# Raw weights in transfers of two blocks, 1 MB each, in place of single blocks of 512 KB

## What is computed

```python
def first_block(x, c, ...):
    for layer in range(2):
        shift_m, scale_m, gate_m, shift_f, scale_f, gate_f = ada_mod(c, ada_w[layer], ada_b[layer])
        h = modulate(rms_norm(x, norm_gains[layer, 0]), shift_m, scale_m)
        y = attn_hybrid_mixer(h, ...) if layer % 2 == 0 else retention_mixer(h, ...)
        x = x + gate_m * y
        h = modulate(rms_norm(x, norm_gains[layer, 1]), shift_f, scale_f)
        x = x + gate_f * swiglu(h, ffn_w_gate_up[layer], ffn_w_down[layer])
    return rms_norm(x, final_norm)

def second_block(x, ...):
    for l in range(2):
        x = hybrid_layer(x, ...)   # convolution, latent attention and dilated attention, gated and merged
    return x
```

## Time and profile before

| | |
|---|---|
| median of 3 runs | 1480.45 us (1480.04 to 1490.38) |
| the profiled execution's own time | 1489.58 us |
| its span, first to last instruction | 1487.6 us |
| TensorE busy | 98% of the span |
| VectorE busy | 70% |
| ScalarE busy | 57% |
| GpSimd busy | 6% |
| mean traffic | 196 GB/s |
| granted TensorE clock, mean | 0.996 of full speed |

### The profile page before, as it was taken

One profiled execution on the slowest core, in us unless ns is written; L12 is line 12 of the kernel. 1 busy time (PEld: TensorE's weight loads), 2 busy tenths in 40 slices (PEclk: granted clock), 3 DMA queues, 4 the chain that ended last, 5 costly groups with the idle time before them and its releaser, 6 DMA issues.

```text
span 1487.6 us, 30216 instructions
## 1 busy us (share of the span) xinstructions
PE 1462.6 (98%) x11596; PEld 1379.8 (93%) x11596; DVE 1037.8 (70%) x1835; ACT 854.3 (57%) x1458; POOL 85.7 (6%) x136
## 2 busy tenths in 40 slices
PE   8999999999999999999999999999999999999999
PEld 6887999999989899999998989889999898989999
DVE  2878888898696666555675857876676674787665
ACT  4565666545456656655566766554566676655553
POOL 0101000110000000000020000220000000021000
PEclk9999999999999999999999999999999999999999
DMA  9966688898574355655663555336666355423663
GB/s 361 329 209 205 224 291 289 291 379 311 186 283 146 123 186 166 185 183 185 186 231 117 164 163 161 96 92 196 194 193 218 103 173 168 149 91 111 191 197 126
DMA packets 81183, 292.02 MB, mean 196 GB/s; under 512 B 9185, under 2 KB 10465, under 8 KB 80946
## 3 DMA queue, kind: packets, MB, share of 16 engines
q1 hardware_dynamic: 68274, 244.31, 50.5%
q0 software_dynamic: 11792, 42.77, 8.7%
q10 hardware_dynamic: 1008, 3.41, 0.7%
HBM read 289.40 MB, written 1.05 MB: 195 GB/s over the span
## 4 chain that ended last, share of the span: by engine, by line
PE 89%; DVE 5%; ACT 3%; issue 2%; DMA 1%; SPq 0%; DVEq 0%; ACTq 0%
PE G L495 22%; PE G L497 22%; PE G L496 22%; PE G L554 2%; PE G L556 2%; PE G L555 2%; DVE wlo L1546 2%; PE O L1037 1%; PE S L1006 1%; PE Tp L962 1%; PE G L576 1%; PE Tp L890 1%; ACT whi L1091 1%; DVE aw L1554 1%; PE G L582 1%
## 5 line engine op out<-in xcount | busy, mean ns | idle before, releaser
L1546 DVE TENSOR_TENSOR wlo<-raw,whi 128x1024 fp32r<-128x1024 f32 x444 | 548.5, 1237 | 282.1 <-ACT whi L1091 279.4
L1091 ACT ACTIVATE whi<-raw 128x1024 fp32r<-128x1024 f32 x444 | 469.1, 1058 | 233.3 <-PE G L497 177.9
L495 PE MATMUL G<-h,whi 128*128 128x256 f32 x2096 | 596.8, 285 | 1.1 <-DVE at L2128 0.7
L497 PE MATMUL G<-h,wlo 128*128 128x256 f32 x2096 | 582.2, 278 | 0.0
L496 PE MATMUL G<-h,whi 128*128 128x256 f32 x2096 | 582.2, 278 | 0.0
L495 PEld LDWEIGHTS G<-h,whi 128*128 128x128 f32 x2096 | 395.6, 189 | 9.6 <-issue 5.9
L496 PEld LDWEIGHTS G<-h,whi 128*128 128x128 f32 x2096 | 394.2, 188 | 1.8 <-issue 0.5
L497 PEld LDWEIGHTS G<-h,wlo 128*128 128x128 f32 x2096 | 393.6, 188 | 0.0
L1554 DVE CUSTOM_DVE_ANT_0 aw<-aw,cs,cols 128x1024 f32<-128x1024 f32 x80 | 102.3, 1280 | 0.0
L495 PE MATMUL G<-ah,whi 128*128 128x256 f32 x352 | 98.0, 278 | 0.0
L496 PE MATMUL G<-ah,whi 128*128 128x256 f32 x352 | 98.0, 278 | 0.0
(11 more groups left out here) (341 smaller groups left out, 2270.4 us busy)
## 6 DMA issues: line engine op xcount, KB each, us to landing
raw<-in_w SPq DMA_DIRECT2D x444, 512.0 KB, 3.7
aw<-in_ada POOLq DMA_DIRECT2D x80, 512.0 KB, 5.3
adaw<-in_ada SPq DMA_DIRECT2D x8, 1024.0 KB, 15.8
sn<-in_uq ACTq DMA_DIRECT2D x2, 768.0 KB, 4.3
x<-in_x SPq DMA_DIRECT2D x1, 1024.0 KB, 5.3
pt<-in_ukv ACTq DMA_DIRECT2D x2, 512.0 KB, 5.4
out<-x SPq DMA_DIRECT2D x4, 256.0 KB, 2.3
dec<-in_dec ACTq DMA_DIRECT2D x1, 512.0 KB, 3.6
```

Of the source, the lines that this page charges most:

```text
L495: pe.matmul(o, wh, mv[:, 0:T], start=(k == 0), stop=False)
L497: ins = pe.matmul(o, wl, mv[:, 0:T], start=False, stop=(k == k_of - 1))
L1091: act.activation(whi[:, s, :], raw[:, s, :], ACT.Copy).then_inc(w_hi, 1)
L1546: dve.tensor_tensor(wlo[:, s, :], raw[:, s, :], whi[:, s, :], ALU.subtract).then_inc(w_lo, 1)
```

## The change

One transfer now carries two blocks, 1 MB. The host array has 222 entries of 128 partitions by 2 by 1024 numbers, so that a pair lies in one run of 8 KB for each partition, in HBM as in `raw`. The four places and their sizes stay, and so do `whi` and `wlo`; there are two landing semaphores in place of four. The transfer of blocks n and n+1 (n even) is issued when block n-3, the later of the two whose places it fills, has been subtracted. Both `hi(n)` and `hi(n+1)` wait for the same landing.

```diff
-        w_raw = [sem(f"w_raw{i}") for i in range(4)]
+        w_raw = [sem(f"w_raw{i}") for i in range(2)]
...
                 if q == 4:
-                    for n in range(4):
-                        sp_.dma_start(raw[:, n, :], a["w"][n]).then_inc(w_raw[n], 16)
+                    for n in range(2):
+                        sp_.dma_start(raw[:, 2 * n:2 * n + 2, :], a["w"][n]).then_inc(w_raw[n], 16)
...
             with sp_.Fori(1, N_BLOCKS // 4) as t:
-                for s in range(4):
+                for s in range(2):
 
-                    sp_.wait_ge(w_lo, t * 4 - 3 + s)
-                    sp_.dma_start(raw[:, s, :], a["w"][t * 4 + s]).then_inc(w_raw[s], 16)
+                    sp_.wait_ge(w_lo, t * 4 - 2 + 2 * s)
+                    sp_.dma_start(raw[:, 2 * s:2 * s + 2, :], a["w"][t * 2 + s]).then_inc(w_raw[s], 16)
...
-                act.wait_ge(w_raw[s], 16 * (n // 4 + 1) + 16 * r4)
+                act.wait_ge(w_raw[s // 2], 16 * (n // 4 + 1) + 16 * r4)
...
     assert w.shape[0] == N_BLOCKS, w.shape
+    w = w.reshape(N_BLOCKS // 2, 2, P, 1024).transpose(0, 2, 1, 3)
```

## The result

The changed kernel took 1507.22 us (median of 4 runs, 1501.41 to 1509.34) where the kernel before took 1483.51 in the same comparison (1480.04 to 1490.38): a ratio of 1.0138 [1.0101, 1.0175], estimated from all runs; by the medians alone it is 1.6%. Run again on another occasion it gave 1.0187 [1.0149, 1.0225]. The forecast was +7.3 us; 23.7 came. It is the first rival ("fallen behind for good", 1502) that the time speaks for, and the profile has to show whether it came by that way.

The account below looks back on a forecast made before the run. The prediction took TensorE, busy 98% of the span, to bound the kernel. Losses of 2.4 + 4.2 + 0.7 = 7.3 us at three places, on the median of 1480.45, gave 1487.8 us (+0.5%), range 1480 to 1497.

Parts of the forecast that it names:

- first rival: Down projection of layer 0 and token projections: crowded transfers fall behind for good, 22 us lost, 1502 us; chance 0.13.
- The bound, and the quiet stretches: TensorE busy 98% of the span; in quiet steady stretches 1 MB lands in 4.8 to 5 us and nothing waits.
- First place: 45 to 76 us: late pairs (8,9) to (12,13) delay TensorE, up to the start of the scores, by 2.4 us.
- Second place: 389 to 440 us, retention projections: late pairs make TensorE lose 1.5 us at block 119 and then 2.7, in sum 4.2.
- Third place: 762 to 772 us, entry of the hybrid part: block 233's result leaves PSUM late, and TensorE loses 0.7 us.
- One landing for two: Every pair: the even block waits for both halves, 1.3 us more; with the later start 4.0 of 5.1 us in hand.
- the 5.8 us on the converted side: Steady state: converted weights are ready 5.8 us before TensorE wants them, claimed to cover raw lateness of 2 us; cost 0.
- the shortfall: Down projection of layer 0: landing at 7.1 us loses 0.9 us a loop, 5 in all, claimed just covered.
- the sign: 302 to 340 us, down projection of layer 0: TensorE waits there would show the forecast wrong; no size given.
- Nothing reaches TensorE: Crowded places: 8 KB packets move raw weights at twice the `aw` rate; only 1 + 1.5 us remain, 1483 us; chance 0.17.
- Bigger transfers win: Raw loads: larger transfers cost less per byte and end standing waits; gain at most 1 us, 1479.5 us; chance 0.03.

Follow-up runs that it names:

- single_again: The kernel before, unchanged, run again for a second profile: 1484.43 us, 1.0007 of the kernel before.
- pair_again: The changed kernel, unchanged, run again for a second profile: 1512.83 us, 1.0187 of the kernel before.
- pair_thin: The changed kernel with conditioning loads behind the fifth cut to 128 of 1024 columns, dot sums zeroed: 1492.06 us, 1.0047 of the kernel before.
- pair4k: The changed kernel with a pair's two blocks apart in HBM, so packets keep 4 KB: 1510.75 us, 1.0183 of the kernel before.
- late_joint: The kernel before, its 512 KB transfers issued at the pair's time, even blocks also waiting for the odd landing: 1512.06 us, 1.0181 of the kernel before.
- late: The kernel before, its single 512 KB transfers both issued only when the changed kernel's pair would start: 1490.73 us, 1.0038 of the kernel before.
- pair_moved: The changed kernel with three of the four rotary pieces on VectorE one block later: 1506.32 us, 1.0168 of the kernel before.
- single_moved: The kernel before with three of the four rotary pieces on VectorE one block later: 1487.36 us, 1.0024 of the kernel before.

## Why the prediction was wrong

*The bound, and the quiet stretches: right.* TensorE's own work did not change, landings are 4.8 us, and the changed kernel lost nothing from block 146 to 227 or from 240 on: 0.0 and 0.1 us against `single_again`. One reading was wrong, without weight in the sum: the 1022 matmuls in 120 us were not records missing from a pace of 2.72 us a block, but a true pace of 2.83 in that profile (last section).

*First place: 2.4 forecast, 3.3 measured.* ScalarE's hi 8 waited for the landing at 54.9 us and hi 10 for one at 61.85; `mqk` is taken out behind it and TensorE waits 2.62 us where it waited 0.52, as the mechanism said. The wait at the scores, the other half of the forecast, is there in `pair_again` (0.77 us; its scores start 2.5 us later than in `single_again`, counted from block 0, where 2.4 was forecast). In the first profile it is hidden by what was missing from the forecast, the clock: 0.59 from 64 to 68 us. TensorE comes to the scores at 74.65 us, when the last rotary operation had ended at 73.97.

*Second place: 4.2 forecast, 7.6 measured.* The mechanism was right to the waiting instruction. ScalarE there:

```profile
430.72 2.01 ACT L1091 ACTIVATE whi<-raw 128x1024 fp32r<-128x1024 f32 x2 [7.37 <-DMA raw<-in_w]
...
437.38 1.06 ACT L1091 ACTIVATE whi<-raw 128x1024 fp32r<-128x1024 f32 x1 [3.93 <-issue]
438.34 0.36 ACT L1124 ACTIVATE rv<-G 128x256 f32<-128x256 f32 x1
```

Hi 122 waits 7.37 us for a transfer that could only start when lo 119 was done, behind the six rotary operations; hi 124 waits too (the trace names no releaser for it, but its transfer could start at 430.11 us, when lo 121 ended, and would land some 7.2 later, about when hi 124 starts), and the evac behind it releases TensorE at 439.21. The stops are 1.21, 0.27 and 3.27 us, 4.75 where 4.2 was forecast. Some 0.4 of the 7.6 are `single_again`'s own, and another 0.43 is a wait for `rqk` at block 113. Most of the rest is again the clock behind the stop, 0.57 from 440 to 444 us. Without the crowd the place costs less: `pair_thin` loses 3.4 here.

*Third place: 0.7 forecast, 0.8 measured.*

*The step that failed* stands under "One landing for two": "Even if the raw side is late by 2 us where `aw` runs beside it, the 5.8 us on the converted side cover it: price nothing", and again in the first rival, "loses 0.9 a loop, 5 in all, just covered". The landing was put right (7.1, measured 7.2), and so was the shortfall (5; VectorE's waits grew by 4.9). But the 5.8 us are what a block's weights have in hand. A norm ends the stretch, its square stands behind two lo's in VectorE's order, and the wait of 1.5 us that it had already said that nothing was in hand there. I looked for the cost as a wait of TensorE for `wlo` between 302 and 340 us, and named that as the sign; it came 20 us later, as a wait for `sq`. With 5 us there, 1.4 for the clock, and 1.7 for the like at the norm at 168 us (there VectorE isn't even full: its last lo before the square waits 2.21 us for a hi that waited 2.53 for its landing), the forecast would have been 7.3 + 8.1 = 15.4 and slower by 1%.

*The rivals.* "Fallen behind for good" was the right one, at 6.4 to 7.8 us in the down projection where it said 9. "Nothing reaches TensorE" leaned on packets of 8 KB getting twice the share; `pair4k` shows no such thing. "Bigger transfers win" rested on "Batch DMAs to ≥1 MiB for ≥75% of peak" in the Trainium skill (page DMA: Bandwidth & Descriptors, section Bandwidth). No run here bears it out for this stream. The raw queue's share of the DMA engines' time did fall, from 50.5% to 45.6%, but it is 45.9% in `late_joint` too, whose pieces are 512 KB; and that kernel takes the pair's time; the later start alone brings it to 46.4% (`late`). What a stream with a deadline wants is an early landing, and 512 KB land after 3.5 us where 1 MB takes 4.8.

*What stays open.* The ledger explains 18.6 us against `single_again`. The medians are 23.7 to 28.3 us apart; the 5 to 10 us between lie, in the profiles that have them, in TensorE's own pace. That pace is seen with single transfers too; whether the pair meets the slower one more often, no run here settles.

## What to carry over

Time in hand is a property of each consumer and not of a stream: beside the block that wants the weights, look for whatever else stands behind the conversion on the same in-order engine, above all the last step before a norm, and take any wait that it shows already as zero in hand. A wait that is put on a full engine (36.56 of 38 us) isn't hidden but handed on nearly whole, and shows later and under another name. Two costs that use up the same time in hand aren't to be added: apart they took 0.4 and 0.6%, together 1.8%.

## What the runs showed of the hardware

*The clock behind a stop.* Stops of TensorE of 2.6, 6.5 and 3.3 us were followed by a lower granted clock: 0.59 in the mean from 64 to 68 us, 0.50 from 360 to 364, 0.57 from 440 to 444. The stops of 1.76 us (at 168 us) and 1.46 us (the norm, kernel before) were not: 1.00. The length of the stop alone doesn't decide it: a stop of 2.48 us in `pair_again` (at `mqk`) and one of 3.40 in `pair_moved` (L847) left it at 1.00. TensorE stops for 1.67 us near 135 us in every profile of this case, and behind it the clock was 0.57 over 4 us in the first profile of the kernel before and 1.00 in `single_again`, the same kernel:

```profile
134.97 0.47 PE L736 MATMUL S<-sp,usum 128*128 128x128 f32 x1 [1.67 <-DVE zs L1652]
```

```profile
135.00:139.00 4.00, 4.00 (x22) 3.07 (x22) 2.86 (x5) 0.52 (x2) 0.27 (x1) 0.57 0.72 252
```

```profile
136.00:140.00 4.00, 3.65 (x31) 2.78 (x32) 3.69 (x6) 1.93 (x5) 0.37 (x1) 1.00 0.72 249
```

The prediction counted stops at their length, though the trace of the kernel before showed the like: the matmul that waited 3.17 us and the window behind it,

```profile
509.29 0.67 PE L847 MATMUL Tp<-sq,ones 128*128 128x256 f32 x2 [3.17 <-DVE sq L1795]
```

```profile
510.00:514.00 4.00, 4.00 (x23) 4.00 (x22) 3.18 (x6) 0.97 (x3) 0.00 (x0) 0.57 0.71 236
```

with 0.57 granted and 23 matmuls in 4 us. A new stop of that length is to be priced with what the clock may take behind it, here some 1 to 2 us where it did.

*TensorE's pace.* With the granted clock at 1.00 throughout, TensorE took 2.72 us a block in some stretches and 2.83 in others. Window 560 to 760 us of the first profile of the kernel before and of the changed kernel:

```profile
560.00:760.00 200.00, 199.04 (x1678) 197.91 (x1677) 118.17 (x163) 115.67 (x165) 0.00 (x0) 1.00 0.57 177
```

```profile
560.00:760.00 200.00, 198.97 (x1739) 197.82 (x1739) 123.61 (x167) 117.38 (x164) 0.00 (x0) 1.00 0.53 190
```

Here the kernel before is the one that runs 4% slower, 8.4 us over blocks 146 to 228 against `single_again`; in `pair_again` it is the pair (6.8 us), and in `single_moved` it is there in two stretches (6.7 and 6.8), the first of them blocks 32 to 96. So executions of both kernels show it, and the edits don't explain it; its cause is open. It is why the two first profiles are only 11.8 us apart, and why the ledger goes by places.
